# When a decay is computed: moving one task in the written-out order of a gated-linear-attention layer

## The reference, cut to what matters

```
def gla_chunk_step(S, inp):
    q, k, v, g = inp
    bcum = jnp.cumsum(g, axis=1)
    decay = jnp.exp(jnp.where(causal, bcum[:, :, None] - bcum[:, None], -jnp.inf))
    attn = jnp.einsum('bihk,bjhk,bijhk->bhij', q, k, decay)
    o = jnp.einsum('bhij,bjhv->bihv', attn, v) + jnp.einsum('bihk,bhkv->bihv', q * jnp.exp(bcum), S)
    k_dec = k * jnp.exp(b_last[:, None] - bcum)
    S = jnp.exp(b_last)[..., None] * S + jnp.einsum('bjhk,bjhv->bhkv', k_dec, v)
    return S, o
...
    o = o * lax.rsqrt(jnp.mean(o * o, axis=-1, keepdims=True) + NORM_EPS)
    o = o.reshape(bsz, l, GLA_DV) * jax.nn.silu(r)
    y = o.astype(h.dtype) @ w_out
```

## Time and profile before

| | us |
|---|---|
| three runs | 1505.68, 1505.78, 1498.8 |
| median | 1505.68 |
| the profiled execution: time | 1505.68 |
| the profiled execution: span | 1503.9 |
| TensorE busy | 1417.1 |
| VectorE busy | 1166.2 |
| ScalarE busy | 839.9 |
| GpSimd busy | 239.0 |

### The profile page before, as it was taken

One profiled execution on the slowest core, in us unless ns is written; L12 is line 12 of the kernel. 1 busy time (PEld: TensorE's weight loads), 2 busy tenths in 40 slices (PEclk: granted clock), 3 DMA queues, 4 the chain that ended last, 5 costly groups with the idle time before them and its releaser, 6 DMA issues. The chain is left out here.

```text
span 1503.9 us, 31302 instructions
## 1 busy us (share of the span) xinstructions
PE 1417.1 (94%) x11554; PEld 1180.0 (78%) x11554; DVE 1166.2 (78%) x2591; ACT 839.9 (56%) x1877; POOL 239.0 (16%) x424
## 2 busy tenths in 40 slices
PE   5999999799999979999999999979999999999987
PEld 5889887667888759988888888767777777777765
DVE  4556587758877986898887898995879777588786
ACT  4745555366556545556665764663746556464453
POOL 5010122001422100121110221120112211000002
PEclk8999999999999979999999999999999999999999
DMA  6474567356576434448844764853585674555463
GB/s 191 126 227 136 169 175 219 98 165 189 140 194 204 123 98 131 144 108 229 240 131 134 238 181 124 243 143 86 168 247 156 161 216 119 167 158 174 132 190 64
DMA packets 283874, 245.77 MB, mean 163 GB/s; under 512 B 32664, under 2 KB 250876, under 8 KB 283052
## 3 DMA queue, kind: packets, MB, share of 16 engines
q1 hardware_dynamic: 273628, 209.36, 47.2%
q0 software_dynamic: 10096, 34.41, 8.7%
HBM read 183.02 MB, written 65.00 MB: 165 GB/s over the span
## 5 line engine op out<-in xcount | busy, mean ns | idle before, releaser
L1482 PE MATMUL bank<-h,w 128*128 128x268 f32 (+1 forms) x4752 | 836.0, 330 | 19.2 <-ACT w L867 13.0
L1482 PEld LDWEIGHTS bank<-h,w 128*128 128x128 f32 x4752 | 701.2, 191 | 96.9 <-issue 22.8
L883 DVE TENSOR_TENSOR w<-w_raw,w 128x1024 fp32r<-128x1024 f32 x132 | 160.9, 1219 | 42.9 <-ACT w L867 42.6
L852 PE MATMUL bank<-s_w_out,s_yt_hi 128*128 128x512 f32 (+2 forms) x544 | 168.1, 398 | 2.0 <-DVE s_ys L2600 1.7
L867 ACT ACTIVATE w<-w_raw 128x1024 fp32r<-128x1024 f32 x132 | 138.7, 1051 | 7.8 <-DMA w_raw<-in_ssd_w_in_dram 7.7
L1560 DVE SCALAR_TENSOR_TENSOR conv<-before_conv,cw,conv 128x260 f32<-128x260 f32 (+2 forms) x216 | 125.3, 580 | 4.3
L852 PEld LDWEIGHTS bank<-s_w_out,s_yt_hi 128*128 128x128 f32 (+2 forms) x544 | 95.9, 180 | 28.6 <-issue 2.5
L852 PE MATMUL bank<-g_w_out,g_ot_hi 128*128 128x512 f32 (+2 forms) x288 | 98.0, 429 | 1.7 <-DVE g_ot_lo L2118 1.7
L852 PE MATMUL bank<-s_w_out,s_yt_lo 128*128 128x512 f32 x240 | 94.7, 395 | 0.0
L2363 ACT ACTIVATE s_decay<-s_decay,t_ac 128x128 f32<-128x128 f32 (+1 forms) x288 | 85.5, 379 | 1.2
L1528 ACT ACTIVATE conv<-bank,cw 128x268 f32<-128x268 f32 (+1 forms) x72 | 45.8, 637 | 67.1 <-PE bank L1482 48.7
(11 more groups left out here) (259 smaller groups left out, 2460.7 us busy)
## 6 DMA issues: line engine op xcount, KB each, us to landing
w_raw<-in_ssd_w_in_dram SPq DMA_DIRECT2D x80, 512.0 KB, 4.3
w_raw<-in_gla_w_in_dram SPq DMA_DIRECT2D x48, 512.0 KB, 4.4
s_decay<-kept_acd SPq DMA_DIRECT2D x32, 512.0 KB, 6.3
w_raw<-in_ssd_w_out_dram SPq DMA_DIRECT2D x30, 512.0 KB, 4.2
g_chunk<-kept_gq SPq DMA_DIRECT2D x32, 448.0 KB, 5.4
s_chunk<-kept_sq SPq DMA_DIRECT2D x32, 384.0 KB, 4.8
kept_sq<-stage SPq DMA_DIRECT2D x80, 134.0 KB, 4.5
kept_sq<-stage SPq DMA_DIRECT2D x40, 256.0 KB, 4.9
```

What stands on the lines that cost most here:

```text
L852: last = pe.matmul(bank[0:r, :], yt[a][:, k, 0:r], wo[:, b, 512 * half:512 * half + 512], start=(k + a + b == 0), stop=(k == tiles - 1 and ...
L883: dve.tensor_tensor(self.part(i, 1), self.raw(i), hi, ALU.subtract).then_inc(self.w_lo, 1)
L1482: last = pe.matmul(bank[:, 0:n], w[:, p.tile % 2, a, k, :], h[:, b, k, c:c + n], start=(i == 0), stop=(i == len(terms) - 1))
```

## The change

In the table `gla`, ("decay", 1) moves two places ahead: from behind ("turn", -1) and ("fill", 0.5) to a place ahead of both, right behind ("keys", 0) and ("levels", 0).

```
-        gla = [("distance", 1), ("keys", 0), ("levels", 0), ("turn", -1), ("fill", 0.5), ("decay", 1), ("load", 2),
+        gla = [("distance", 1), ("keys", 0), ("levels", 0), ("decay", 1), ("turn", -1), ("fill", 0.5), ("load", 2),
```

## The result

| | before | after |
|---|---|---|
| median of 8 runs (lowest to highest), us | 1503.53 (1498.8 to 1505.78) | 1512.74 (1508.55 to 1515.9) |
| ratio, 95% interval | | 1.0057 [1.0045, 1.007] |
| profiled execution, time / span, us | 1505.68 / 1503.9 | 1508.13 / 1506.4 |

The kernel is 0.57% slower, 8.6 us [6.8, 10.5]; the forecast was 1514 us and "slower by over 0.5%". So the profiles are used for where time went, and the medians for how much.

The account below looks back on a forecast made before the run. TensorE bounds 291 to 500 us, VectorE 250 to 291 and 500 to 561 us, with little reserve in either from 650 to 700. Seven terms sum to 8.7 us on 1505.68 us, forecast 1514 us; 8-in-10 range 1503 to 1523.

Parts of the forecast that it names:

- 1, 193 us: At 193 us, VectorE's stall of 0.57 us for a small g_ot_hi partly reaches TensorE, which waits for g_attn: +0.4 us.
- 2, 250 to 291 us: Three events where VectorE sets the pace: its stalls reach TensorE through waits for y_acc and h, +1.6 us.
- 3, 320 us: At 320 us, table load and decay come ahead of g_ot_hi and evacuation L1164; L1172 frees a PSUM bank late: +0.65 us.
- 4, 350 us: At 350 us, ScalarE idles for the distance and a block comes behind the decay, delaying TensorE's weight split L867: +1.15 us.
- 5, 366 us: At 366 us, weight split L867 comes behind the decay and is ready at 370.35, its tile starting at 368.81: +1.6 us.
- 6, 500 to 561 us: Five events where VectorE sets the pace: stalls of 0.37, 0.75, 0.75, 0.55 and 0.4 us reach TensorE, +2.8 us.
- 7, 631 us: At 631 us, an evacuation behind the decay frees its bank late; TensorE loses 2.6 us, mostly regained: +0.5 us taken.
- VectorE's stall: VectorE waits at g_ot_lo for g_ot_hi, now behind the decay: 0.7 to 0.75 us in about 20 events, 24 us in all.
- the clock: Rival, 8%: more waiting brings another stretch of low granted clock, looked for in 500 to 561 us: 1517 to 1520 us.
- covered: Rival, 25%: queues absorb stalls of 0.7 us; only the 350 and 366 us delays and part of 500-561 arrive: 1509 us.
- not slower: Rival, 10%: evacuations and splits up to 1 us earlier feed TensorE's waits for w, at most 4.5 us less: 1501 us.
- all through: Rival, 12%: VectorE's stalls add up even where TensorE is busy, some events from 380 to 430 us; bound 1530, half 1520.

Follow-up runs that it names:

- f3: Decay moved in nine events only (193 us, three of 250 to 291 us, five of 500 to 561 us), against the kernel before: ratio 1.003, +4.5 us.
- g1: Decay moved only in the three events at 320, 350 and 366 us, against the kernel before: ratio 1.0018, +2.7 us.
- f1: Decay moved only in the one event at 609 us, against the kernel before: ratio 1.0, 0.0 us.
- f2: Decay moved only in the one event at 631 us, against the kernel before: ratio 1.0014, +2.1 us.
- e1: Decay moved ahead of the fill only, still behind g_ot_hi (the turn), against the kernel before: ratio 1.0046, +6.9 us.
- g2: Decay moved the other way, one place back behind the event's second fill, against the kernel before: 1497.64 us against 1501.68, ratio 0.9976.
- e3: Decay moved only in the five events at 320, 350, 366, 609 and 631 us, against the kernel before: ratio 1.0041, +6.2 us.

## Why the prediction was right, step by step

The sum of the prediction against the steps of TensorE's shift, each against the one trace of before:

| term | predicted | in the profile after | in a part alone |
|---|---|---|---|
| 1, 193 us | 0.4 | 0.2 | 0.2 (f3) |
| 2, 250 to 291 us | 1.6 | 1.0 | 1.2 (f3) |
| 3, 320 us | 0.65 | 0.57 | 0.57 (g1) |
| 4, 350 us | 1.15 | 0.4 | 0.4 (g1), but 0.4 in f1 too |
| 5, 366 us | 1.6 | 1.42 | 1.41 (g1) |
| 6, 500 to 561 us | 2.8 | 1.25, then -0.8 | 1.73, then -0.2 (f3) |
| 7, 631 us | 0.5 | 3.2 | 1.85 (f2) |
| sum | 8.7 | 7.3 | |

The medians of the parts are the better measure of how much:

| terms | predicted | by medians |
|---|---|---|
| 1, 2 and 6 | 4.8 | 4.5 [2.9, 6.0] (f3) |
| 3, 4 and 5 | 3.4 | 2.7 [0.3, 5.1] (g1) |
| 7 | 0.5 | 2.1 [0.5, 3.8] (f2) and 0.0 (f1, the event at 609 us) |
| sum | 8.7 | 9.3 in parts, 8.6 [6.8, 10.5] in the whole kernel |

The size came out right, the mechanism too; but term 7 was too small and term 4 too large.

**VectorE's stall.** Predicted at 0.7 to 0.75 us in each of about 20 late events; the trace has 0.69 to 0.73 in 17. Predicted behind the sample step 1.7 us, twice, and 3.7 once; measured 1.52, twice, and 4.63. Predicted in all 24 us (12 to 24 us in some 25 events); 24.0 us in 30, of which 21.8 in 26 are g_ot_lo's. The working by starts and ends of a few rows held because every duration in it was measured and no engine's list but one changed.

**Terms 3 and 5** hold to 0.2 us. In both, what TensorE needs came behind a wait, and the price was the difference between its new end and the start of the piece. For term 3, L1172 now ends at 327.03 and TensorE waits 0.50 us for the bank. Counting 24 matmuls to a tile told which piece it is.

**Term 4** was counted as if term 3 had not happened. ScalarE's split starts at 355.11 in place of 354.37. ScalarE's g_k_turned ahead of it came 0.42 us earlier than before in this trace, so the decay delays the split by 1.16 us, as predicted. But TensorE, 0.57 us late since 320 us, waits only 0.63 us for it, in place of 0.22 (0.22 to 0.36 in the kernels that move nothing there). e1 has no loss at 320 us, and there the same wait is 1.40 us, 1.0 to 1.2 more than where nothing is moved: term 4 by itself. Two delays that end at the same engine give about the larger one, not the sum: 1.0 for both in place of 1.8.

**Term 6** looks too large in the table and probably is not. Its first three events were put at 0.37, 0.75 and 0.75. TensorE was later by 0.0 behind the first (511 us), by 0.9 at 521 us and 0.35 more at 532: the stalls are there (0.71 at 503.76, 0.72 at 515.11, 0.71 at 527.06), but a part of them does not reach TensorE in this pair. The last two, put at 0.95 together, gave -0.8 in this execution and -0.2 in f3. There the time also hangs on the clock: from 500 to 561 us the granted clock was 0.86 before, 0.94 after and 0.89 in f3, with the same lists on TensorE. So this term can't be read from one trace to better than 2 to 3 us. Against unmoved kernels at the same clock it is 2.4 to 3.8 us (under f3), and the median of f3 agrees.

**Term 7 is the mis-sized one**: 0.5 predicted, 3.2 measured. Its steps were: the bank is freed 2.6 us too late (measured 2.48 alone, 3.64 in the whole kernel, since the event at 609 us was left out); most of this comes back in the reserve of 4.0 of 50 us from 650 us on (measured: 2.6 come back; of the 4.0 us only 2.2 lie ahead of 694 us, the rest is the wait for w at the border of 700 us). What failed is that a wait of TensorE was priced by its length alone. The granted clock fell behind it, and the piece cost 2.1 us more. The rows show the sizes: behind 1.20 us (g1, 367.95) the 12 matmuls took 3.00 us (0.25 each, against 0.28 in the earlier trace rows) at a granted clock of 1.00; behind 2.48 and 3.64 us the clock was 0.56 and 0.55 over the next 5 us. The Trainium skill (TensorE: Matmul & The Clock Gate, The HAM clock gate) has TensorE throttled unless its activity releases the clock; the clock of 0.55 and 0.56 behind the two waits agrees with that. The prediction had this as its rival "the clock" (8%), but looked for it from 500 to 561 us, where the stretches are slow anyway, and not at the one place where a busy TensorE at 1.00 was to be stopped for more than 2 us.

So the sum is right in part by luck. Term 7 is 1.6 us too small by the medians of its parts and 2.7 by the trace of the whole kernel; terms 3 to 5 are too large by 0.7 us (medians) or 1.0 (trace); terms 1, 2 and 6 are within 0.3 us by the median, with 1.5 us of uncertainty. The errors partly cancel, and the line of 0.5%, which the forecast gave only 52%, was passed by 0.07%, less than the uncertainty of 0.12%. Two of the signs of being right did not come as written: the wait for w grew by 1.5 us, not 2 to 3, and TensorE's idle time from 250 to 291 us fell from 11.5 to 10.8 us; the window holds other instructions then, for TensorE's shift is -1.8 us at 250 and +1.3 at 291.

Of the rivals, "covered" is refuted by f3, "not slower" by the ratio, and "all through" by the flat shift from 387 to 511 us: VectorE's stalls went on there in every late event, and TensorE ran without a delay.

## What to carry to other kernels

In a list that an engine runs strictly in order, an instruction that waits for a late input is charged to everything behind it: place it where its input is ready, not where its engine is free. To price such a move, list what it passes and find for each passed instruction the engine that needs it and the time to spare (banks and copies, too); delays that meet at one engine give the largest, not the sum. And where a wait stops a matrix engine that was busy until then, look at the granted clock behind the stop: here it added 2 us to a wait of 2.5 at 631 us, and nothing to one of 2.6 us at 292.

## What the runs showed that I had not expected

The same lists of TensorE run at a different granted clock from one execution to the next in stretches with gaps: from 530 to 545 us it was 0.66 before and in g1, 0.79 in f1, 0.89 in f2 and g2. Before, f1, f2 and g1 have the same order of all engines in this stretch:

```profile
530.00:545.00 15.00, 11.89 (x97) 9.15 (x97) 12.29 (x32) 5.82 (x15) 1.92 (x3) 0.66 0.68 206
```

```profile
530.00:545.00 15.00, 10.58 (x99) 8.15 (x98) 13.11 (x39) 5.47 (x12) 0.74 (x2) 0.89 0.76 232
```

The first is before, the second f2: 10.6 us of matmuls in place of 11.9 for as many instructions. Between 532 and 572 us f2's shift goes from -1.52 to -4.53 with nothing changed there. Two single traces of this kernel can differ by 2 to 3 us in such a place, as much as any one term of the prediction. The steps at 320, 366 and 631 us of after come again in e3 to 0.15 us; those of the two slow borders do not, and there only several kernels at a like clock, or the medians, tell a term's size.
